# State space stage: products over 32 rows, real and imaginary output in two banks and column groups, the weight's rest in the middle of a state tile

## The reference

```python
proj = u @ w_in                      # u_ssm, q, k, v, xq and three gates
uf = u_ssm.reshape(bsz, seqlen, 32, 16)
bu_re = jnp.einsum('blgh,gph->blgp', uf, bbar_re)
bu_im = jnp.einsum('blgh,gph->blgp', uf, bbar_im)
_, _, x_re, x_im = lax.associative_scan(combine, (a_seq_re, a_seq_im, bu_re, bu_im), axis=1)
y = (jnp.einsum('blgp,ghp->blgh', x_re, c_re)
     - jnp.einsum('blgp,ghp->blgh', x_im, c_im) + uf * d_skip)
```

## Time and profile before

| | |
|---|---|
| median of 3 runs | 2571.93 us (2571.05 to 2572.59) |
| the profiled execution | 2573.01 us, span 2571.2 us |
| granted TensorE clock, mean | 0.998 |
| PE busy | 2532.8 us, 99% |
| DVE busy | 1327.0 us, 52% |
| ACT busy | 940.8 us, 37% |
| POOL busy | 412.6 us, 16% |
| chain that ended last | PE 88%, DVE 5%, ACT 3%, issue 2% |

### The profile page before, as it was taken

How to read it: one execution, slowest core, us unless ns; L and a number is a source line. 1 busy time by engine, 2 the same in 40 slices (tenths; PEclk the granted TensorE clock), 3 DMA queues, 4 the chain that set the end, 5 groups by cost and what they waited for, 6 DMA issues and landing times.

```text
span 2571.2 us, 30674 instructions
## 1 busy us (share of the span) xinstructions
PE 2532.8 (99%) x11844; PEld 2003.6 (78%) x11844; DVE 1327.0 (52%) x1695; ACT 940.8 (37%) x1328; POOL 412.6 (16%) x358
## 2 busy tenths in 40 slices
PE   9999999999999999999999999999999999999998
PEld 7866788887875788888788888877776678888886
DVE  7764632435966452342633332699963567433322
ACT  4344532323344442232422232444345454322221
POOL 1201000001111100001111101287711320111101
PEclk9999999999999999999999999999999999999999
DMA  4301222222321222222222232411231043222232
GB/s 158 144 34 66 82 98 98 98 98 82 132 83 35 80 98 98 88 94 104 80 94 97 90 107 102 173 66 66 86 132 46 25 156 125 88 98 98 84 101 78
DMA packets 40999, 241.72 MB, mean 94 GB/s; under 512 B 4800, under 2 KB 5312, under 8 KB 17984
## 3 DMA queue, kind: packets, MB, share of 16 engines
q1 hardware_dynamic: 39760, 232.95, 25.5%
q0 software_dynamic: 560, 5.24, 0.5%
q10 hardware_dynamic: 576, 2.10, 0.2%
HBM read 231.88 MB, written 8.39 MB: 93 GB/s over the span
## 4 chain that ended last, share of the span: by engine, by line
PE 88%; DVE 5%; ACT 3%; issue 2%; DMA 0%; POOL 0%; DVEq 0%; ACTq 0%; SPq 0%
PE gemm L439 75%; ACT w_hi L368 1%; PE gemm L623 1%; PE gemm L624 1%; PE gemm L632 1%; DVE x_sb L584 1%; PE score L1713 1%; PE mixed L1724 1%; PE score L1771 1%; PE gemm L1830 1%; DVE out_sb L538 1%; PE score L835 1%; PE turned L1785 1%; PE mixed L488 1%; PE turned L846 1%
## 5 line engine op out<-in xcount | busy, mean ns | idle before, releaser
L377 DVE TENSOR_TENSOR w_lo<-w_raw,w_hi 128x2048 fp32r<-128x2048 f32 (+2 forms) x207 | 442.1, 2136 | 569.3 <-ACT w_hi L368 569.2
L439 PE MATMUL gemm<-h_hi,w_hi 128*128 128x512 f32 x1776 | 705.1, 397 | 0.8 <-ACT u_sb L1984 0.5
L439 PE MATMUL gemm<-h_hi,w_lo 128*128 128x512 f32 x1776 | 692.8, 390 | 0.0
L439 PE MATMUL gemm<-h_lo,w_hi 128*128 128x512 f32 x1776 | 692.0, 390 | 0.0
L368 ACT ACTIVATE w_hi<-w_raw 128x2048 fp32r<-128x2048 f32 (+3 forms) x217 | 381.7, 1759 | 401.4 <-PE gemm L439 361.5
L439 PEld LDWEIGHTS gemm<-h_hi,w_lo 128*128 128x128 f32 x1776 | 333.6, 188 | 70.5
L439 PEld LDWEIGHTS gemm<-h_hi,w_hi 128*128 128x128 f32 x1776 | 334.1, 188 | 69.7 <-issue 2.3
L439 PEld LDWEIGHTS gemm<-h_lo,w_hi 128*128 128x128 f32 x1776 | 334.2, 188 | 67.3 <-issue 1.7
L439 PE MATMUL gemm<-f_hi,w_hi 128*128 128x512 f32 x512 | 199.2, 389 | 0.0
L439 PE MATMUL gemm<-f_lo,w_hi 128*128 128x512 f32 x512 | 199.2, 389 | 0.0
L439 PE MATMUL gemm<-f_hi,w_lo 128*128 128x512 f32 x512 | 199.2, 389 | 0.0
(11 more groups left out here) (398 smaller groups left out, 3709.5 us busy)
## 6 DMA issues: line engine op xcount, KB each, us to landing
w_raw<-in_w SPq DMA_DIRECT2D x171, 1024.0 KB, 4.7
w_raw<-in_w SPq DMA_DIRECT2D x16, 768.0 KB, 4.0
w_raw<-in_w SPq DMA_DIRECT2D x16, 640.0 KB, 3.7
w_raw<-in_w SPq DMA_DIRECT2D x18, 512.0 KB, 3.5
bias_t<-in_att_bias SPq DMA_DIRECT2D x2, 1536.0 KB, 8.5
decay_t<-in_c_decay SPq DMA_DIRECT2D x2, 1536.0 KB, 9.2
x_sb<-in_x SPq DMA_DIRECT2D x4, 512.0 KB, 6.8
x_kept<-x_sb SPq DMA_DIRECT2D x1, 2048.0 KB, 12.2
```

The lines of the kernel that those rows point to most:

```text
L377: dve.tensor_tensor(w_lo[:, b.slot, 0:size], w_raw[:, b.slot, 0:size], w_hi[:, b.slot, 0:size].bitcast(F32), ALU.subtract).then_inc(S["w_r ...
L439: mm = pe.matmul(dst, lhs, rhs, start=b.first and k == 0 and j == 0, stop=b.last and k == b.kt - 1 and j == 2)
```

## The change

- Scan input: B is turned once for four state tiles (`turn_b(a)`), and each matmul takes only the 32 rows of its state tile: rows 32t for the real part, and for the imaginary part rows 32(t + 2 mod 4), for which GpSimd's DMA keeps a copy of u with its halves swapped (`u_roll`). The turn stands in the slots 1, 5 and 9.
- Scan output: C has 32 columns a tile. The real part goes to 32 partitions of mixed, the imaginary part to other 32 partitions of gemm3, each matmul on its own without accumulation over tiles. The gemm tiles of the 15 pieces (and of no others) go round three banks instead of four, so that gemm3 is free.
- VectorE: `skip` adds the imaginary half from gemm3 in two further instructions of 64 partitions. The cosine products of tile s move from the end of `scan(s)` to behind the rotations of `scan(s + 1)`. The rest of the weight moves from behind the scans to behind the state sum.
- GpSimd: ten larger copies at the start in place of eight small ones for each tile; two roll DMAs for each of the first two groups of u before its first phase, and two more behind the sines of tiles 4 and 8.
- ScalarE: 4 copies of the turned B instead of 16.

```diff
     for b in pieces:
         b.t0 = sum(groups[:b.g])
-        b.bank = 0 if b.narrow else 2 * (b.g % 2)
         if b.first:
-            banks = [b.bank + (m if b.kind == "feat" else m // 2) for m in range(b.tiles)]
+            bank = 2 * b.g % 3 if b.three else 0 if b.narrow else 2 * (b.g % 2)
+            banks = [bank + (m if b.kind == "feat" else m // 2) for m in range(b.tiles)]
+            if b.three:
+                banks = [q % 3 for q in banks]
             b.need = [last_tile[q] for q in banks]
             for m, q in enumerate(banks):
                 last_tile[q] = b.t0 + m + 1
+        b.banks = banks
-            out.append(Piece(0, c, WCOLS, KD, "feat" if name == "v" and c > col else kind, "w_in2"))
+            out.append(Piece(0, c, WCOLS, KD, "feat" if name == "v" and c > col else kind, "w_in2",
+                             three=name != "u"))
...
-        b_mat = at("b_mat", [P, 4, 2, P], F32, FZ + 68)
-        c_mat = at("c_mat", [P, 4, 2, P], F32, FZ + 72)
+        b_all = at("b_all", [P, 2, STILES // 4, 4, SSM_G * 2], F32, FZ + 68)
+        c_all = at("c_all", [P, 2, STILES, SSM_G * 2], F32, FZ + 72)
+        u_roll = at("u_roll", [P, 2, SEQ], F32, FZ + 62)
...
+        def rows_of(s, j):
+            t = (s % 4 + 2 * j) % 4
+            return slice(2 * SSM_G * t, 2 * SSM_G * t + 2 * SSM_G)
...
-            def turn_b(s):
-                pe.wait_ge(S["mats"], 8 * (s + 1))
-                if s:
-                    pe.wait_ge(S["bt_s"], s)
+            def turn_b(a):
+                if a:
+                    pe.wait_ge(S["bt_s"], a)
+                else:
+                    pe.wait_ge(S["mats"], MATS)
                 if values[0]:
                     pe.wait_ge(S["values_kept"], values[0])
-                turned_b[0] = s + 1
+                turned_b[0] = a + 1
                 for j in range(2):
-                    mm = pe.transpose(t_ps[:, P * j:P * j + P], b_mat[:, s % 4, j, :], ident[:])
+                    mm = pe.transpose(t_ps[:, P * j:P * j + P], b_all[:, j, a].rearrange("p t c -> p (t c)"), ident[:])
                 mm.then_inc(S["turned_b"], 1)
             def scan_in(s):
-                pe.wait_ge(S["bt_s"], s + 1)
+                a = s // 4
+                if s % 4 == 0:
+                    pe.wait_ge(S["bt_s"], a + 1)
+                    pe.wait_ge(S[f"rolled{a % 2}"], 32 * (a // 2 + 1))
                 if s:
                     pe.wait_ge(S["bu_read"], s)
-                for j in range(2):
-                    mm = pe.matmul(s_ps[j][:], b_turned[:, s % 2, P * j:P * j + P], u_sb[:, s // 4, :],
-                                   start=True, stop=True)
+                for j, u in enumerate((u_sb[:, a, :], u_roll[:, a % 2, :])):
+                    r = rows_of(s, j)
+                    mm = pe.matmul(s_ps[j][:], b_turned[r, a % 2, P * j:P * j + P], u[r], start=True, stop=True)
                 mm.then_inc(S["bu_ps"], 1)
             def scan_out(s):
                 pe.wait_ge(S["state_s"], s + 1)
                 if s % 4 == 0:
                     pe.wait_ge(S["y_read"], s // 4) if s else pe.wait_ge(S["norm_log"], N0 + 2)
-                for j in range(2):
-                    mm = pe.matmul(o_ps[:], c_mat[:, s % 4, j, :], state[:, s % 2, j, :],
-                                   start=s % 4 == 0 and j == 0, stop=s % 4 == 3 and j == 1)
+                for j, to in enumerate((o_ps, bank[3])):
+                    mm = pe.matmul(to[rows_of(s, j)], c_all[:, j, s, :], state[:, s % 2, j, :], start=True, stop=True)
...
-                        if s + 1 < STILES:
-                            turn_b(s + 1)
+                        if s % 4 == 1 and s + 3 < STILES:
+                            turn_b(s // 4 + 1)
...
-            pool.memset(b_mat[:], 0.0).then_inc(S["mat_zero"], 1)
-            pool.memset(c_mat[:], 0.0).then_inc(S["mat_zero"], 1)
+            pool.memset(b_all[:], 0.0).then_inc(S["mat_zero"], 1)
+            pool.memset(c_all[:], 0.0).then_inc(S["mat_zero"], 1)
             pool.wait_ge(S["mat_zero"], 2)
             pool.wait_ge(S["bbar_s"], 3)
-            def mats(s):
-                b = s % 4
-                if s >= 4:
-                    pool.wait_ge(S["turned_b"], s - 3)
-                    pool.wait_ge(S["y_ps"], s - 3)
-                for q in range(2):
-                    r = slice(SSM_N * q, SSM_N * q + SSM_N)
-                    c = slice(32 * b + 16 * q, 32 * b + 16 * q + 16)
-                    f = slice(SSM_G * s, SSM_G * s + SSM_G)
-                    for j in range(2):
-                        pool.tensor_copy(b_mat[r, b, j, c], bbar[r, j, f]).then_inc(S["mats"], 1)
-                        pool.tensor_copy(c_mat[r, b, j, c], (bc[r, 2, f], bbar[r, 3, f])[j]).then_inc(S["mats"], 1)
+            def roll(a):
+                pool.wait_ge(S["g_free"], plan2[AT2["u"]].t0 + a + 1)
+                if a >= 2:
+                    pool.wait_ge(S["bu_ps"], 4 * (a - 1))
+                for r in range(2):
+                    to, src = slice(HD * (1 - r), HD * (1 - r) + HD), slice(HD * r, HD * r + HD)
+                    pool.dma_start(u_roll[to, a % 2, :], u_sb[src, a, :]).then_inc(S[f"rolled{a % 2}"], 16)
+            for q in range(2):
+                r = slice(SSM_N * q, SSM_N * q + SSM_N)
+                c = slice(SSM_G * q, SSM_G * q + SSM_G)
+                of_tile = lambda a: a.rearrange("p (a t c) -> p a t c", t=4, c=SSM_G)
+                re, im = of_tile(bbar[r, 0, :]), of_tile(bbar[r, 1, :])
+                pool.tensor_copy(b_all[r, 0, :, :, c], re).then_inc(S["mats"], 1)
+                for half in range(2):
+                    to, src = slice(2 - 2 * half, 4 - 2 * half), slice(2 * half, 2 * half + 2)
+                    pool.tensor_copy(b_all[r, 1, :, to, c], im[:, :, src, :]).then_inc(S["mats"], 1)
+                by_tile = lambda a: a.rearrange("p (s c) -> p s c", c=SSM_G)
+                pool.tensor_copy(c_all[r, 0, :, c], by_tile(bc[r, 2, :])).then_inc(S["mats"], 1)
+                pool.tensor_copy(c_all[r, 1, :, c], by_tile(bbar[r, 3, :])).then_inc(S["mats"], 1)
+            pool.wait_ge(S["mats"], MATS)
+            for a in range(2):
+                roll(a)
...
             for s in range(STILES):
-                if s + 2 < STILES:
-                    mats(s + 2)
-                    pool.wait_ge(S["mats"], 8 * (s + 3))
                 sines(s)
+                if s in (4, 8):
+                    roll(s // 4 + 1)
...
-            def copy_b(s):
-                act.wait_ge(S["turned_b"], s + 1)
-                if s >= 2:
-                    act.wait_ge(S["bu_ps"], s - 1)
-                act.activation(b_turned[:, s % 2, :], t_ps[:, 0:2 * P], ACT.Copy).then_inc(S["bt_s"], 1)
+            def copy_b(a):
+                act.wait_ge(S["turned_b"], a + 1)
+                if a >= 2:
+                    act.wait_ge(S["bu_ps"], 4 * (a - 1))
+                act.activation(b_turned[:, a % 2, :], t_ps[:, 0:2 * P], ACT.Copy).then_inc(S["bt_s"], 1)
...
+            def cosines(s):
+                if s == 0:
+                    dve.wait_ge(S["x_kept_s"], 16)
+                if s >= 2:
+                    dve.wait_ge(S["y_ps"], s - 1)
+                for w in range(2):
+                    dve.wait_ge(S["scanned"], 2 * s + w + 1)
+                    dve.tensor_tensor(state[:, s % 2, w, :], z_sc[:, s % 2, w, :], trig[:, s % 2, 0, :],
+                                      ALU.mult).then_inc(S["z_cos_s"], 1)
...
+                    cosines(s - 1)
                     state_sum(s - 1)
                 if s >= 5 and s % 4 == 1:
                     skip(s // 4 - 1)
+                if rest is not None:
+                    rest_block(dve, rest)
                 phase_step(s + 1, 0)
...
-                if rest is not None:
-                    rest_block(dve, rest)
-                if s == 0:
-                    dve.wait_ge(S["x_kept_s"], 16)
-                if s >= 2:
-                    dve.wait_ge(S["y_ps"], s - 1)
-                for w in range(2):
-                    dve.wait_ge(S["scanned"], 2 * s + w + 1)
-                    dve.tensor_tensor(state[:, s % 2, w, :], z[w], cos, ALU.mult).then_inc(S["z_cos_s"], 1)
             def skip(a):
                 dve.wait_ge(S["y_ps"], 4 * a + 4)
                 dve.scalar_tensor_tensor(out=u_sb[:, a, :], in0=u_sb[:, a, :], scalar=ssm_d[:, a:a + 1], in1=o_ps[:],
-                                         op0=ALU.mult, op1=ALU.add).then_inc(S["y_read"], 1)
+                                         op0=ALU.mult, op1=ALU.add).then_inc(S["real_read"], 1)
+                dve.wait_ge(S["real_read"], a + 1)
+                for r in range(2):
+                    to, src = slice(HD * r, HD * r + HD), slice(HD * (1 - r), HD * (1 - r) + HD)
+                    add = dve.tensor_tensor(u_sb[to, a, :], u_sb[to, a, :], bank[3][src], ALU.add)
+                    add.then_inc(S["y_read"] if r else S["half_read"], 1)
```

(6 more changed lines are left out.)

28 lines of the change are left out of this document (14 added, 14 removed).

## The result

| | before | changed |
|---|---|---|
| median (20 runs each) | 2571.65 us (2569.9 to 2573.24) | 2575.63 us (2573.32 to 2576.64) |
| the profiled execution | 2573.01 us, span 2571.2 | 2575.99 us, span 2573.9 |
| PE busy / DVE / POOL | 2532.8 / 1327.0 / 412.6 us | 2518.7 / 1318.8 / 337.0 us |
| last state sum done | 1889.91 us | 1894.05 us |

The ratio is 1.0013, with a 95% interval of 1.0007 to 1.0019: 4.0 us slower, where 2 us faster was forecast. That is under the 0.2% that the prediction called the limit of telling, but twenty runs of each do tell it from none.

What follows compares the result with a forecast made beforehand. TensorE and VectorE were both full in the state space stage, VectorE deciding. Legs -6.0, end +0.9, first tile and rolls +1.8, clock +1.3 gave -2.0 us; 2573.0 - 2.0 - 1.1 = 2570.0, range 2560 to 2580.

Steps and rivals of the forecast that it cites:

- TensorE's 24 us: State space stage: overlapping matmul pairs and fewer turns of B shrink TensorE's work by about 24 us, 22 becoming waits.
- The early legs: VectorE's rotations-to-rotations distances in early tiles: 12.4 us for 0 to 1, 14.8 each for 1 to 4, 10.7 for 4 to 5.
- The legs with the rest in the middle: Six VectorE legs, tiles 6 to 9 and 10 to 13, weight's rest ahead of the clamp: 12.9 us each.
- The term for the cosines: VectorE's two cosine products, moved ahead of the clamp and so inside the loop, cost 1.2 us a leg.
- the prediction's own sign of being wrong: Wrong if TensorE stays without waits, or if GpSimd's phase steps and VectorE's sums stretch each other.
- The skip legs: VectorE legs with skip's two added half-tile adds: 15.0 us for 5 to 6 and 9 to 10, 16.9 for 13 to 14.
- the later rolls: GpSimd's two roll DMAs before a later phase, at about 1 us an issue: 1.0 us together.
- Given back: Costs set against shorter legs: stage end +0.9, tile 0's start and rolls +1.8, clock behind TensorE's last wait +1.3 us.
- The row against the rule: A trace row had GpSimd's phase step delay VectorE by 0.1 us; the skill's exclusive port lock was set aside.
- the slower rival: GpSimd in VectorE's way behind the rotations: 1.3 us in each of eight legs, tiles 5 to 13; 2580 us, chance 0.20.
- The clock rival: Every TensorE wait over 2 us is followed by 1.2 GHz, making TensorE late: 5 us more, 2575, chance 0.06.
- Pairs that do not overlap: TensorE's matmul pairs gain no overlap, VectorE binds anyway: 1.4 us more for the last two outputs, 2571, chance 0.06.

Runs made afterwards that it cites:

- experiment 7: Changed kernel with both matmuls of a pair on the same 32 rows (scan input) or in the same 32 columns (scan output): 2578.82 us.
- experiment 9: Changed kernel without the two half-tile adds in skip: 2571.09 us.
- experiment 3: Changed kernel with cosines and the weight's rest both back behind the scans, new products kept: 2572.81 us.
- experiment 5: Changed kernel with cosines back behind the scans, and both phase steps and the clamp directly behind rotations and state sum: 2570.51 us.
- experiment 6: The kernel of experiment 5 with GpSimd also writing the whole turns one tile further ahead, before the tile's z_sin: 2561.99 us.
- experiment 8: Changed kernel without the rolled copy of u and its DMAs; the second scan input matmul reads u itself: 2572.97 us.
- experiment 1: Changed kernel with the two cosine products back behind the scans, the weight's rest staying in the middle: 2570.14 us.

## Why the prediction was wrong

*What bounds the kernel.* Right: two engines were full, and VectorE decides once TensorE has less to do (experiments 7 and 9); that GpSimd's phase can stand in the same loop (experiments 3, 5 and 6) is not in the prediction's sum.

*TensorE's 24 us.* Right: pairs at 1.06 and 0.98 for 1.01, slots at 2.04 for 2.1; experiment 7 puts the price of no overlap at 24 us of work. As forecast it became waits, the named ones and some not named (the turn of the values for ScalarE, 3.0), 18.5 us in all, and the rest a lower clock in the stage (0.97).

*The early legs.* Right within 0.15: 12.46, 14.85 and 10.83 for 12.4, 14.8 and 10.7.

*The legs with the rest in the middle, forecast 12.9.* **This is the step that failed.** They measured 13.48 to 13.55. The term for the cosines, 1.2 us, is where most of it lies: contention with GpSimd's phase step was put at nothing in it, on the strength of the earlier trace rows, and they show 1.72 to 1.78 there (1750.90 to 1752.61 in the leg shown, 0.5 more than the term). The six such legs make 3.8 of the 8.1 by which the sum of legs was missed. The mean of one cosine instruction, forecast near 0.65, is 0.80 (1.19 before), and the prediction's own sign of being wrong came true: the phase step and VectorE's products stretched each other.

*The skip legs, forecast 15.0, 15.0 and 16.9.* Low by 1.5, 1.5 and 0.9, together 3.9, of which 1.0 had been put in apart, as the price of the later rolls. Skip takes 2.35 us, not 2.1 (1737.90 to 1740.25). Most of the rest is the same contention: in the legs with roll DMAs GpSimd's phase comes later and meets the state sum as well, which takes 2.11 for 1.28.

*Given back.* The end: 15.2 for 15.0. Tile 0: 0.9 for 0.8. The later rolls: 1.2 by experiment 8, for 1.0, with some luck: no price stood in the trace before, "about 1 us an issue" was twice too much (GpSimd shows two issues at 1.11), and the legs pay through the contention that the delay moves. The clock: behind the last wait of TensorE (2.87 us, about 3 forecast) the window of 1896 to 1898 shows it at its lower level, 0.50:

```profile
1894.00:1896.00 2.00, 1.81 (x6) 0.90 (x7) 0.76 (x2) 1.86 (x2) 0.00 (x0) 0.81 0.56 214
1896.00:1898.00 2.00, 2.00 (x6) 1.52 (x6) 1.75 (x4) 1.97 (x3) 0.00 (x0) 0.50 0.16 55
1898.00:1900.00 2.00, 2.00 (x9) 1.62 (x8) 0.88 (x1) 2.00 (x4) 0.00 (x0) 0.84 0.47 154
```

0.19, 0.50 and 0.16 of 2 us each are 1.7 us lost, for 1.3. But the drop of the earlier trace rows, behind a wait of 2.05 us of the next stage, did not come again after the same wait (granted 1.00 from 1919 to 1925), which gave about as much back. So a term of 1.3 was put in where the balance is about 0. Left out of the sum was the last pair of products, 0.7 shorter behind the last state sum.

*The whole.* By the prediction's terms the last state sum should have come 3.3 us earlier (legs -6.0, tile 0 +0.8, rolls +1.0, end +0.9); it came 4.1 later. Of this miss of 7.4, contention with GpSimd in legs 5 to 14 that had no price is about 4.6 (seven legs at 0.5 and two at 1.1 make 5.6 or 5.7, less the 1.0 for the rolls), the longer skip 0.8, and about 2 are spread over all terms at 0.1 or so each. Behind the stage 1.3 was too much and 0.7 missing, and 0.7 came back untraced.

*The row against the rule.* I took the row, a tenth of a microsecond of contention. What was measured is 0.5 in a plain middle leg and 1.1 with a roll in it (1.55 and 2.11 for 1.28 each): between the row and the 1.3 that I had given the slower rival for each of eight legs. The row was the wrong one to rest on, because it shows one kind of meeting only. A rest and a phase step, in experiment 1, hold each other up for about the whole of what is left of the first (3.40 for 1.49). z_sin, 2.55 in the changed kernel's legs, took 5.67 at the end of the stage beside the last rest and cosines. The Trainium skill, SBUF — State Buffer, Who interferes with whom, calls the shared port pair an exclusive lock held for the whole instruction. By that rule the second comer waits for the first to end; the rest against the phase step agrees. The cosines agree in kind, not in size: the first phase step had only 0.23 left (it ends at 1751.13), and where their records stand apart (leg 13 to 14) the second cosine takes most of the stretch, 1.09 for 0.68, yet ends 0.3 before the second phase step does. The state sums of the earlier trace rows, begun 0.4 into such a step and 0.1 longer, do not agree at all; no run here tells why.

*The rivals.* The slower one (GpSimd in VectorE's way, 2580, 0.20) had the right mechanism and about twice the size: the contention in legs 5 to 14 comes to some 5.6 us, not 10, and is the largest part of what turned -2 into +4. My 0.20 was too little for it. The clock rival (0.06, 2575) gives the right number for a wrong reason, since experiment 7 has no low clock in the stage up to the last wait and is slower. Pairs that do not overlap: 1.4 on top of the forecast was given for it, and experiment 7 is 2.0 over the changed kernel.

## What to carry to other kernels

Where two engines are equally full, a saving on one may be worth little until the other's loop is shortened too: here the new products (with their adds and rolls) in the old order gave +1.1 us, the order of experiment 6 with the old products +0.9, and both together -10.8. In a loop over two engines count what stands ahead of the hand-over, and let the helpers (here GpSimd's whole turns) work one iteration ahead. Expect a VectorE step with both operands in SBUF and a GpSimd step to hold each other up (a step by 0.1 to 2.1 us in the cases shown here), and price each new meeting by the widest stretch that the trace shows, not by a mild one.

## What the runs showed of the hardware, unexpected

- A VectorE subtraction of 128 x 2048 (2.28 us) stretched a GpSimd step from 1.49 to 3.40 us (experiment 1), and was itself stretched by 0.4 by the step ahead of that one. In the changed kernel's early legs GpSimd's first phase step takes 2.75 beside it, and 0.69 in the middle legs.
- The rotations (VectorE, one operand in PSUM) ran beside z_sin in the changed kernel, and both kept their times, 0.6 a rotation and 2.55 for two.
- Two float32 matmuls on different 32-row strips, or in different 32-column groups with outputs in two banks, start 0.01 us apart and take 1.06 and 0.98 as a pair; on one strip or in one group 1.91 and 1.83 (experiment 7).
- Two DMA issues on GpSimd's queue took 1.11 us of that engine (1733.88), and its phase stands behind them, at 1735.03.
- A wait of TensorE of 2.05 us was followed by the lower clock in one run (0.50 from 1916 to 1918, before) and not in the other (1.00 from 1919 to 1925, changed), with the same instructions around it. The changed kernel had been at the lower clock 20 us earlier; no run tells whether that matters.
